# Two merged transformer layers on one core: index-head weights inside a projection panel, paired index scores, a first panel in pieces, and an output made token by token

## The chip, the cores and the metric

One core of a Trainium2 chip runs the whole kernel, in one launch. The metric is the device time in microseconds; smaller is better. A run's time lies some 2 us above the span that its trace shows from the first to the last instruction.

## The reference, cut to what matters

Input x has 512 tokens of width 1024, all in fp32. A first layer (sliding-window and differential attention, then a feed-forward part with a short convolution) is followed by a second one:

```python
xn = rms_norm(x, norm_gain)
z = xn @ w_in
q, c_kv, q_idx, k_idx, w_idx, g_attn, x_rnn, g_rnn, merge = split_cols(z)   # 1024,128,512,64,8,1024,1024,1024,2048
c_kv = rms_norm(c_kv, kv_norm_gain)
k_idx = layer_norm(k_idx, idx_ln_gain, idx_ln_bias)
s_idx = relu(einsum('btjd,bsd->btjs', q_idx, k_idx))          # 8 index heads of width 64
s_idx = einsum('btjs,btj->bts', s_idx, w_idx)                 # causal, then the 128 best keys of each token
o = attention over the chosen keys, 16 heads
mixed = sigmoid(merge_a) * ((o * silu(g_attn)) @ w_attn_proj) + sigmoid(merge_r) * (rg_lru(...) @ w_rnn_proj)
x = x + mixed @ w_out
return rms_norm(x, final_norm_gain)
```

The norm at the end is over the width of each token. The matrix products run in a split form: each operand is a rounded fp32 high part and a low part, and a product is three matmuls, high x high, high x low, low x high.

## The kernel before

**Panels.** All weights come as 100 panels of 128 x 2048 fp32 (1 MB), in the order of `STAGES`: in1 (3), fill1, out1, the feed-forward stages up0 to dn3, then in2a (7), xr, rg, wr, ga, mga, ap, out2 (4). SyncE loads panel p into `RAW[p % 2]`, one transfer each, once the low half of panel p - 2 is done. ScalarE rounds it to the high half `WH` (`hi`, L889; for panel p + 2 when TensorE has finished panel p: `hi_ahead`). VectorE (L1341) or, for stages not in `LO_STAGES`, GpSimd (L334, four pieces) makes the low half `WL`. TensorE's `one_panel` (L341) does 48 matmuls of 128x512 per panel: two output tiles m, eight chunks c of the contraction, three passes (L354 to L356). Its outputs are two of the four banks of `PG`, alternating with the panel, and a panel begins when its low half is there and the panel two before it is evacuated by VectorE. Where `ready` is given the order is chunk by chunk, so that each chunk of the activations (high `XH` by ScalarE, low `XL` by VectorE) can arrive while the panel runs.

**The start.** SyncE issues the columns `COL` (200 KB of vectors), panel 0, two slices of x, panel 1; ScalarE issues the other two slices of x. TensorE waits for panel 0 to land, runs 14 warm-up matmuls (`keep_warm`, L406), then panel 0. ScalarE squares x (L951), VectorE adds the four pairs (`add_pairs`, L1318) and TensorE sums over the partitions with two fp32 matmuls against a constant (`mean_square`, L400), after panel 0. `factor` turns the sum into R, by which every evacuation is multiplied. The norms n3 and n5 do the same a quarter of the way into the second panel that follows.

**in2a.** Panel 0 of in2a holds the latent and, twice, the index key (64 columns and their copy); panels 1 and 2 the index queries, 3 to 6 the queries. After panel 1 TensorE does `kv_sums` (mean of the key, mean square of the latent), `w_idx` (the eight index weights of all tokens, 24 matmuls with 8 output columns, L708 to L710) and `ln_sums`. `idx_scores(u)` (L743 to L745) is one index head of one block of 128 query tokens: three matmuls on 64 rows against 256, 384 or 512 keys. The 24 units stand one by one after the chunks of panels 3 and 4 that `IDX_PLACES` names; ScalarE takes the relu from four `PX` banks (L1165) and VectorE adds it, weighted, to the mask `MD` (L1745).

**The attention scores** (`mla_scores`, L822) of a head pair are two fp32 matmuls, one on rows 0 to 63 and one on rows 64 to 127, into different banks. An fp32 matmul leaves two records.

**The end.** ap (L354 with `RH`, `OLO`) gives the attention's part; VectorE gates it (L1990), adds the recurrence's part (L1993) and makes the low part (L1328). out2 has features on the partitions: VectorE adds x, reloaded into `XT` (L2001), ScalarE squares; after the last panel come four mean-square matmuls with warm-up ones between them, the logarithm and exponential of `factor`, and eight scalings `SQ2` (L2005) with a store for every two.

**The form of dn3.** The last feed-forward stage puts tokens on the partitions (`down_panel`): each of two column halves is two panels, each with half the contraction, and the token tiles end one after the other in the second. VectorE adds a tile (L1716), ScalarE squares it with a running sum (L930) and takes the root (L945), and VectorE's `token_factor` makes the tile's factor (L1568 to L1574).

## Time and profile before

| | |
|---|---|
| three runs | 1342.82, 1342.91, 1340.68 us, median 1342.82 |
| the profiled execution | 1342.5 us, span 1340.4 us |
| TensorE busy | 1312.2 us (98%), granted clock 0.996 of full |
| VectorE, ScalarE, GpSimd busy | 838.2, 576.4, 217.1 us |
| high half of a panel, ScalarE | 1.91 us |
| low half of a panel | 2.29 us on VectorE, 5.0 to 6.8 us on GpSimd |
| a slice of x, 128x512 | 0.71 us high (ScalarE), 0.75 us low (VectorE) |
| last low parts before out2 (L1328) | 1282.41 to 1289.29 |

Each time in the trace counts from the first instruction. One engine that is busy nearly all of the span sets the end; the others matter where TensorE waits for them. Matmuls are pipelined: the distance of their starts is their cost, and the duration of one (0.39 us for 128x512) is longer than that.

### The profile page before, as it was taken

How to read it: one execution, taken by the hardware profiler on the slowest of the kernel's cores; microseconds unless marked ns; L12 is line 12 of the kernel's file. 1: busy time of each engine (PE TensorE's matmuls, PEld its weight loads, DVE VectorE, ACT ScalarE, POOL GpSimd, SP SyncE). 2: the span in 40 equal slices, each digit the busy share in tenths (PEclk: the TensorE clock that was granted, in tenths of full speed). 3: DMA queues.
4: the chain of work that ended last, by engine and by line, in shares of the span. 5: the costliest groups of instructions: out<-in, count | busy, mean ns of one | idle time of the engine just before them, and what ended most of it. 6: DMA issues, size and time to landing. Idle time of an engine off the chain costs nothing.

```text
span 1340.4 us, 16043 instructions
## 1 busy us (share of the span) xinstructions
PE 1312.2 (98%) x5982; PEld 1023.7 (76%) x5982; DVE 838.2 (63%) x1450; ACT 576.4 (43%) x871; POOL 217.1 (16%) x173
## 2 busy tenths in 40 slices
PE   7999998999999999999999999999999999999996
PEld 6777677888888888888888876687778866668885
DVE  6455765898887388648853554688886356642333
ACT  5344766544443244224422463224573256654221
POOL 1333320000000000000000032340005411123550
PEclk9999999999999999999999999999999999999998
DMA  5211111232222222222222140322122210002411
GB/s 199 95 63 64 34 61 63 73 116 94 94 94 94 94 94 98 103 107 99 96 95 94 63 158 32 126 94 95 63 98 90 95 64 32 32 33 95 157 64 63
DMA packets 17787, 116.51 MB, mean 87 GB/s; under 512 B 1984, under 2 KB 2240, under 8 KB 4544
## 3 DMA queue, kind: packets, MB, share of 16 engines
q1 hardware_dynamic: 16320, 108.35, 22.8%
q10 hardware_dynamic: 1408, 7.37, 1.5%
q8 instruction: 38, 0.62, 0.2%
q14 instruction: 21, 0.17, 0.0%
HBM read 111.52 MB, written 4.19 MB: 86 GB/s over the span
## 4 chain that ended last, share of the span: by engine, by line
PE 97%; ACT 1%; DVE 1%; DMA 0%; issue 0%; DVEq 0%; ACTq 0%; SPq 0%
PE PG L354 19%; PE PG L356 19%; PE PG L355 19%; PE PX L506 5%; PE PX L793 4%; PE PG L441 2%; PE PX L441 2%; PE PX L440 2%; PE PG L442 2%; PE PG L440 2%; PE PX L442 2%; PE PG L822 2%; PE PX L832 1%; PE PX L689 1%; PE PG L574 1%; PE PX L520 1%
## 5 line engine op out<-in xcount | busy, mean ns | idle before, releaser
L354 PE MATMUL PG<-XH,WH 128*128 128x512 f32 x992 | 393.1, 396 | 2.7 <-DVE XL L1606 2.7
L334 POOL TENSOR_TENSOR WL<-RAW,WH 128x512 fp32r<-128x512 f32 x160 | 213.8, 1369 | 1090.7 <-ACT WH L889 1090.7
L355 PE MATMUL PG<-XL,WH 128*128 128x512 f32 x992 | 386.2, 389 | 0.0
L356 PE MATMUL PG<-XH,WL 128*128 128x512 f32 x992 | 386.2, 389 | 0.0
L889 ACT ACTIVATE WH<-RAW 128x2048 fp32r<-128x2048 f32 x100 | 191.4, 1914 | 346.1 <-PE PG L356 234.4
L354 PEld LDWEIGHTS PG<-XH,WH 128*128 128x128 f32 x992 | 186.2, 188 | 48.6 <-issue 10.0
L355 PEld LDWEIGHTS PG<-XL,WH 128*128 128x128 f32 x992 | 186.3, 188 | 39.2 <-issue 1.9
L356 PEld LDWEIGHTS PG<-XH,WL 128*128 128x128 f32 x992 | 186.2, 188 | 38.9
L1341 DVE TENSOR_TENSOR WL<-RAW,WH 128x2048 fp32r<-128x2048 f32 x60 | 137.2, 2287 | 61.0 <-ACT WH L889 60.9
L1094 ACT ACTIVATE Z<-Z 128x512 f32<-128x512 f32 x32 | 20.3, 633 | 164.8 <-DVE Z L1657 164.8
L1641 DVE TENSOR_TENSOR U<-PG,R 128x1024 f32<-128x1024 f32 x32 | 39.2, 1224 | 51.5 <-PE PG L356 46.0
L440 PE MATMUL PX<-WH,AH 128*128 128x512 f32 x128 | 49.8, 389 | 0.0
L441 PE MATMUL PX<-WH,AL 128*128 128x512 f32 x128 | 49.8, 389 | 0.0
L442 PE MATMUL PX<-WL,AH 128*128 128x512 f32 x128 | 49.8, 389 | 0.0
L440 PE MATMUL PG<-WH,AH 128*128 128x512 f32 x128 | 49.8, 389 | 0.0
L441 PE MATMUL PG<-WH,AL 128*128 128x512 f32 x128 | 49.8, 389 | 0.0
L442 PE MATMUL PG<-WL,AH 128*128 128x512 f32 x128 | 49.8, 389 | 0.0
L354 PE MATMUL PG<-RH,WH 128*128 128x512 f32 x128 | 49.8, 389 | 0.0
L356 PE MATMUL PG<-RH,WL 128*128 128x512 f32 x128 | 49.8, 389 | 0.0
L1082 ACT ACTIVATE C<-U,COL 128x512 f32<-128x512 f32 x64 | 48.2, 800 | 0.1
L1652 DVE SCALAR_TENSOR_TENSOR C<-U,COL,C 128x510 f32<-128x510 f32 x64 | 45.1, 747 | 3.8
L1648 DVE SCALAR_TENSOR_TENSOR C<-U,COL,C 128x511 f32<-128x511 f32 x64 | 45.0, 744 | 0.0
(311 smaller groups left out, 2015.9 us busy)
## 6 DMA issues: line engine op xcount, KB each, us to landing
RAW<-panels SPq DMA_DIRECT2D x100, 1024.0 KB, 4.8
x_spill<-XT ACTq DMA_DIRECT2D x1, 2048.0 KB, 7.0
XT<-x_spill ACTq DMA_DIRECT2D x1, 2048.0 KB, 7.9
outT<-SQ SPq DMA_DIRECT2D x4, 512.0 KB, 3.0
XT<-xT ACTq DMA_DIRECT2D x2, 512.0 KB, 6.3
XT<-xT SPq DMA_DIRECT2D x2, 512.0 KB, 8.8
RGW<-rgw ACTq DMA_DIRECT2D x1, 1024.0 KB, 4.8
UK<-uk ACTq DMA_DIRECT2D x1, 512.0 KB, 5.7
```

Source lines behind the costliest of these rows:

```text
L334: ins = pool.tensor_tensor(WL[:, s].rearrange("p a b -> p (a b)")[:, piece], RAW[:, s, piece], WH[:, s].rearrange("p a b -> p (a b)")[:, p ...
L354: pe.matmul(o, WH[:, s, c, ms], xh[:, c, :], start=(c == 0), stop=False)
L355: pe.matmul(o, WH[:, s, c, ms], xl[:, c, :], start=False, stop=False)
L356: mm = pe.matmul(o, WL[:, s, c, ms], xh[:, c, :], start=False, stop=(c == DC - 1))
L440: pe.matmul(o, ah, wh, start=(half == 0 and c == 0), stop=False)
L441: pe.matmul(o, al, wh, start=False, stop=False)
L442: mm = pe.matmul(o, ah, wl, start=False, stop=(half == 1 and c == 3))
L506: mm = pe.matmul(PX[:, 2, :], w[:, s, c, m * P:(m + 1) * P], x[:, c, :], start=(c == 0 and w is WH and x is XH), stop=(c == DC - 1 and w i ...
L793: mm = pe.matmul(PX[:, 2, :], w[:, s, c, m * P:(m + 1) * P], x[:, c, :], start=(c == 0 and w is WH and x is XH), stop=(c == DC - 1 and w i ...
L889: act.activation(WH[:, s].rearrange("p a b -> p (a b)"), RAW[:, s, :], ACT.Copy).then_inc(w_hi, 1)
L1082: ins = act.activation(C[:, b, m, :], U[:, b, m, :], ACT.Identity, bias=col("cb", k + 32 * m), scale=col("cw2", k + 32 * m))
L1341: dve.tensor_tensor(WL[:, s].rearrange("p a b -> p (a b)"), RAW[:, s, :], WH[:, s].rearrange("p a b -> p (a b)").bitcast(F32), ALU.subtrac ...
```

## The change

- **in2a.** The first panel's columns are the latent, the index key once, the eight index weights and 56 zeros. `w_idx` and its loads and splits go. VectorE evacuates the latent, copies the key to both row halves and scales the weights out of the panel. `kv_sums` moves inside panel 1, behind 39 of its 48 matmuls, `ln_sums` behind 12 matmuls of panel 2. ScalarE's squares stand ahead of the high half of panel 3.
- **Index scores.** A visit does two heads, on the two row halves, with the three passes interleaved; 12 visits.
- **The mean squares.** VectorE adds the last two tiles too, and one matmul sums them. For n1 it moves from behind panel 0 to behind 12 matmuls of panel 1.
- **The start.** Panel 0 comes in three pieces (512, 512 and 1024 columns), with high and low halves per piece; the columns and three slices of x are issued by ScalarE. Sixteen warm-up matmuls wait for the constants alone. The high half of panel 2 stands ahead of the first norm's factor on ScalarE. The recurrence's scales (`lru_scales`, some 20 small operations on VectorE) move behind the first evacuation.
- **The end.** out2 has the form of dn3. Reloaded x is transposed by TensorE during panels 2 and 3 of ap (16 transposes each), ScalarE copies it to `X3T`, and the gain comes as a 128 x 1024 tile. Each token tile is scaled by its own factor and stored in two halves of 256 KB. The output leaves as 512 x 1024, without the host's transposition.

```diff
-        IDX_PLACES = {3: {4 + n: n for n in range(12)}, 4: {2 + n: 12 + n for n in range(12)}}
+        IDX_PLACES = {3: {4 + 2 * n: n for n in range(6)}, 4: {2 + 2 * n: 6 + n for n in range(6)}}
...
-            sp.dma_start(COL[:], cols_in).then_inc(loaded_c, 16)
-            sp.dma_start(RAW[:, 0, :], panels[0]).then_inc(raw_in[0], 16)
-            for k in range(0, 4, 2):
-                sp.dma_start(XT[:, 2 * k:2 * k + 2, :], xT_chunks(k)).then_inc(loaded_x[k], 16)
+            for q in range(3):
+                piece = slice(512 * q, 512 * q + 512 if q < 2 else 2048)
+                sp.dma_start(RAW[:, 0, piece], panels[0][:, piece]).then_inc(raw_in[0] if q == 2 else first_in[q], 16)
+            sp.dma_start(XT[:, 4:6, :], xT_chunks(2)).then_inc(loaded_x[2], 16)
...
+                        if first and c == 2:
+                            pe.wait_ge(once("first_lo"), 2)
+                        if first and c == 4:
+                            pe.wait_ge(w_lo, 1)
...
-                sums = {0: lambda: mean_square(norm, [(acc, 1, src[:, 0, :]), (acc, 1, src[:, 1, :])])}
+                sums = {0: lambda: mean_square(norm, [(acc, 1, src[:, 0, :])])}
...
-            keep_warm(14)
-            gemm_norm("in1", "n1", SQ1, "x1_split")
+            keep_warm(16)
+            acc1 = once("n1_acc")
+            pe.wait_ge(once("first_lo"), 1)
+            one_panel(0, 0, ready=(once("x1_split"), 0), first=True)
+            one_panel(1, 1, quarter_done=lambda: mean_square("n1", [(acc1, 1, SQ1[:, 0, :])]))
...
 
-            def w_idx():
-
-                pe.wait_ge(once("wi_split"), 1)
-                for c in range(DC):
-                    o = PX[0:8, 0, :]
-                    pe.matmul(o, WIH[:, c, :], XH[:, c, :], start=(c == 0), stop=False)
-                    pe.matmul(o, WIL[:, c, :], XH[:, c, :], start=False, stop=False)
-                    mm = pe.matmul(o, WIH[:, c, :], XL[:, c, :], start=False, stop=(c == DC - 1))
-                mm.then_inc(once("wx_ready"), 1)
...
+
+                qb, pair = v // 4 + 1, v % 4
                 n = (qb + 1) * P
-                rows = slice((j % 2) * HD, (j % 2) * HD + HD)
-                if u == 0:
+                if v == 0:
                     pe.wait_ge(once("idx_split"), 2)
-                if u == 3:
+                if v == 1:
                     pe.wait_ge(once("idx_split"), 3)
...
-                    pe.wait_ge(once("idx_relu"), u - 3)
-                qh, ql = (q[rows, j // 2, qb * P:(qb + 1) * P] for q in (QIH, QIL))
-                pe.matmul(PX[:, u % 4, 0:n], qh, KIH[rows, 0:n], start=True, stop=False)
-                pe.matmul(PX[:, u % 4, 0:n], qh, KIL[rows, 0:n], start=False, stop=False)
-                pe.matmul(PX[:, u % 4, 0:n], ql, KIH[rows, 0:n], start=False, stop=True).then_inc(once("idx_s"), 1)
+                if v >= 2:
+                    pe.wait_ge(once("idx_relu"), 2 * v - 2)
+                for k, (q, key) in enumerate(((QIH, KIH), (QIH, KIL), (QIL, KIH))):
+                    for m in range(2):
+                        rows = slice(m * HD, (m + 1) * HD)
+                        mm = pe.matmul(PX[:, (2 * v + m) % 4, 0:n], q[rows, pair, qb * P:(qb + 1) * P], key[rows, 0:n],
+                                       start=(k == 0), stop=(k == 2))
+                        if k == 2:
+                            mm.then_inc(once("idx_s"), 1)
 
             p0 = FIRST["in2a"][0]
             acc = once("n5_acc")
             one_panel(p0, p0 % 2, ready=(once("x3_split"), 0), chunk_done=turn_rest("n4", F4, "x3_new"))
             one_panel(p0 + 1, (p0 + 1) % 2,
-                      quarter_done=lambda: mean_square("n5", [(acc, 1, SQF[:, 0, :]), (acc, 1, SQF[:, 1, :])]))
-            kv_sums()
-            w_idx()
-            ln_sums()
-            one_panel(p0 + 2, p0 % 2)
+                      quarter_done=lambda: mean_square("n5", [(acc, 1, SQF[:, 0, :])]), inner=(1, 4, kv_sums))
+            one_panel(p0 + 2, p0 % 2, quarter_done=ln_sums)
...
-            gemm_sums("out2", "n6", GA, ready=(once("m_split"), 0))
+
...
+
+
+                def turn():
+                    if f == 0:
+                        pe.wait_ge(reloaded, 16)
+                    else:
+                        pe.wait_ge(once("x3_copied"), NB)
+                    for t in range(NB):
+                        for c in range(4):
+                            mm = pe.transpose(PX[:, t, c * P:(c + 1) * P], XT[:, 4 * f + c, t * P:(t + 1) * P], IDN[:])
+                        mm.then_inc(once("x3_turned"), 1)
+
+                return turn
+
+            def last_panel(k):
+
+                p = FIRST["out2"][0] + k
+                f, half = divmod(k, 2)
+                pe.wait_ge(w_lo, p + 1)
+                if k < 2:
+                    pe.wait_ge(once("m_split"), 4 * k + 4)
+                if half == 0:
+                    if f == 0:
+                        pe.wait_ge(once("x3_copied"), 2 * NB)
...
+
+            p0 = FIRST["ap"][0]
+            for k in range(4):
+                one_panel(p0 + k, (p0 + k) % 2, RH, OLO, ready=(once("o_split"), 0) if k == 0 else None,
+                          quarter_done=turn_x3(k - 2) if k >= 2 else None)
+            for k in range(4):
...
+            act.dma_start(COL[:], cols_in).then_inc(loaded_c, 16)
+            for k in (0, 1, 3):
                 act.dma_start(XT[:, 2 * k:2 * k + 2, :], xT_chunks(k)).then_inc(loaded_x[k], 16)
...
+                if k < 2:
+                    act.wait_ge(first_in[k], 16)
+                    act.activation(WH[:, 0, 2 * k:2 * k + 2, :].rearrange("p a b -> p (a b)"),
+                                   RAW[:, 0, 512 * k:512 * k + 512], ACT.Copy).then_inc(once("first_hi"), 1)
+                if k == 2:
+                    act.wait_ge(raw_in[0], 16)
+                    act.activation(WH[:, 0, 4:8, :].rearrange("p a b -> p (a b)"), RAW[:, 0, 1024:2048], ACT.Copy).then_inc(w_hi, 1)
...
             hi(1, 1, 0)
-            squares("n1", SQ1, XT)
+            squares("n1", SQ1, XT, (1, 2, 3))
+            hi_ahead(0)
 
             act.wait_ge(once("lam_dot"), 2)
...
             act.wait_ge(once("ln_x"), 1)
             act.activation(CSQ[:, 1, :], KC[:], ACT.Square).then_inc(once("ln_sq"), 1)
+            hi_ahead(p0 + 1)
...
+                if t in (1, 2):
+                    f = t - 1
+                    if t == 1:
+                        act.dma_start(FG[:], fin_in).then_inc(loaded_f, 16)
+                    for b in range(NB):
+                        act.wait_ge(once("x3_turned"), 4 * f + b + 1)
...
+                    link(dve.tensor_tensor(sq[:, 0:2, :], sq[:, 0:2, :], sq[:, 2 * k:2 * k + 2, :], ALU.add))
+                dve.tensor_tensor(sq[:, 0, :], sq[:, 0, :], sq[:, 1, :], ALU.add).then_inc(once(name + "_acc"), 1)
...
+            for k in range(2):
+                dve.wait_ge(once("first_hi"), k + 1)
+                dve.tensor_tensor(WL[:, 0, 2 * k:2 * k + 2, :].rearrange("p a b -> p (a b)"), RAW[:, 0, 512 * k:512 * k + 512],
+                                  WH[:, 0, 2 * k:2 * k + 2, :].rearrange("p a b -> p (a b)").bitcast(F32), ALU.subtract)\
...
 
-            in2a_out(0, CKV[:])
-            dve.wait_ge(once("wi_hi"), 1)
-            dve.tensor_tensor(WIL[:], WIR[:], WIH[:].bitcast(F32), ALU.subtract).then_inc(once("wi_split"), 1)
-            in2a_out(1, two(QI, 0))
+            dve.wait_ge(panel_done, p0 + 1)
+            dve.tensor_tensor(CKV[:, 0, :], PG[:, 2 * (p0 % 2), :], R[:], ALU.mult).then_inc(once("kv_raw"), 1)
+            for half in (0, HD):
+                ins = dve.tensor_tensor(CKV[half:half + HD, 1, :], PG[0:HD, 2 * (p0 % 2) + 1, :], R[0:HD, :], ALU.mult)
+            ins.then_inc(once("ki_raw"), 1)
+            dve.scalar_tensor_tensor(out=WXT[HD:HD + 8, :], in0=PG[HD:HD + 8, 2 * (p0 % 2) + 1, :],
+                                     scalar=IDX_HEADS ** -0.5 * HD ** -0.5, in1=R[HD:HD + 8, :],
+                                     op0=ALU.mult, op1=ALU.mult).then_inc(evac, 1)
             dve.wait_ge(once("ln_mean"), 1)
-            dve.wait_ge(evac, p0 + 1)
+            dve.wait_ge(once("ki_raw"), 1)
             dve.scalar_tensor_tensor(out=KC[:], in0=PX[:, 3, :], scalar=-1.0, in1=CKV[:, 1, :],
                                      op0=ALU.mult, op1=ALU.add).then_inc(once("ln_x"), 1)
+            in2a_out(1, two(QI, 0))
             dve.wait_ge(once("qi_hi"), 1)
             dve.wait_ge(evac, p0 + 2)
...
-                dve.scalar_tensor_tensor(out=SQ2[:, c, :], in0=M2[:, c, :], scalar=col("final", c), in1=R[:],
-                                         op0=ALU.mult, op1=ALU.mult).then_inc(once("out_ready"), 1)
+            dve.wait_ge(once("x3_copied"), 2 * NB)
+            for m in range(2):
+                if m == 0:
+                    dve.wait_ge(once("dn_tile"), 26)
+                else:
...
+            def store(t, f):
+                fs = slice(f * S, (f + 1) * S)
+                dve.scalar_tensor_tensor(out=OT[:, t, fs], in0=X3T[:, t, fs], scalar=RTK[:, 3 * t + 2:3 * t + 3],
+                                         in1=FG[:, fs], op0=ALU.mult, op1=ALU.mult).then_inc(once("out_ready"), 1)
+
+            for t in range(NB):
+                if t < 3:
+                    dve.wait_ge(once("dn_tile"), 28 + t)
+                else:
+                    dve.wait_ge(panel_done, p0 + 4)
+                dst = X3T[:, t, S:]
+                dve.scalar_tensor_tensor(out=dst, in0=PG[:, t, :], scalar=0.5, in1=dst, op0=ALU.mult, op1=ALU.add)\
+                    .then_inc(once("tok_y") if t < 3 else evac, 1 + t // 3)
+                if t == 1:
+                    first_half("n6")
+                    dve.wait_ge(loaded_f, 16)
+                if t in (1, 2):
+                    token_factor("n6", t - 1)
+                    store(t - 1, 0)
+                    store(t - 1, 1)
+            token_factor("n6", 2)
+            store(2, 0)
+            token_factor("n6", 3)
+            store(3, 0)
+            store(3, 1)
+            store(2, 1)
 
...
+        panel(np.concatenate([ckv, ki, wi, np.zeros((1024, 56), np.float32)], 1)), panel(qi), panel(q2), panel(xr), inter(gr, mg[:, 1024:]), panel(a["w_rnn_proj_2"]),
+        panel(ga), panel(mg[:, :1024]), panel(a["w_attn_proj_2"]), halves(a["w_out_2"]),
```

## Rows read from the trace of the kernel before

**Rows 1.** The page, part 4: the chain that ended last, by engine.
```profile
PE 97%; ACT 1%; DVE 1%; DMA 0%; issue 0%; DVEq 0%; ACTq 0%; SPq 0%
```

**Rows 2.** Timeline of VectorE in ap: start us, us, instruction, xcount, idle before.
```profile
1269.07 1.22 DVE L1990 SCALAR_TENSOR_TENSOR SG<-MGA,PG 128x1024 f32<-128x1024 f32 x1 [4.93 <-PE PG L356]
...
1279.94 1.22 DVE L1990 SCALAR_TENSOR_TENSOR SG<-MGA,PG 128x1024 f32<-128x1024 f32 x1 [4.92 <-PE PG L356]
```

**Rows 3.** Timeline of the start.
```profile
1.33 0.29 POOL L307 TENSOR_SCALAR_AFFINE_SELECT IDN<-IDN 128x128 f32<-128x128 f32 x1 [0.24 <-POOL IDN L305]
...
8.01 5.31 PE L406 MATMUL PX<-O 128*128 128x128 f32 x28 [8.01 <-DMA RAW<-panels]
...
10.16 5.02 ACT L971 ACTIVATE XH<-XT,COL 128x512 fp32r<-128x512 f32 x8 [0.35 <-DMA XT<-xT]
...
13.08 0.47 PE L354 MATMUL PG<-XH,WH 128*128 128x512 f32 x1
...
19.55 3.74 DVE L1318 TENSOR_TENSOR SQ<-SQ 128x1024 f32<-128x1024 f32 x3
```

**Rows 4.** Busy time per stretch: PE, PEld, DVE, ACT, POOL; clock, DMA share, GB/s.
```profile
8.50:9.00 0.50, 0.50 (x4) 0.50 (x3) 0.00 (x0) 0.50 (x1) 0.00 (x0) 1.00 1.06 401
...
4.00:5.00 1.00, 0.00 (x0) 0.00 (x0) 0.00 (x0) 0.00 (x0) 0.41 (x3) 1.00 1.08 426
```

**Rows 5.** DMA issues of 0 to 40 us: count, size, median us to landing.
```profile
COL<-cols SPq DMA_DIRECT2D x1, 200.0 KB, 3.0
```

**Rows 6.** Timeline around the mean square of n5.
```profile
776.18 3.74 DVE L1318 TENSOR_TENSOR SQF<-SQF 128x1024 f32<-128x1024 f32 x3
...
780.91 1.88 PE L400 MATMUL PX<-SQF,O 128*128 128x512 f32 x4
...
782.86 0.40 PE L355 MATMUL PG<-XL,WH 128*128 128x512 f32 x1
```

**Rows 7.** Timeline of TensorE between panels 1 and 2 of in2a.
```profile
790.84 1.02 PE L715 MATMUL PX<-CKV,O 128*128 128x512 f32 x2
...
799.20 0.40 PE L355 MATMUL PG<-XL,WH 128*128 128x512 f32 x1
```

**Rows 8.** Timeline of ScalarE: the second step of the factor R for n5.
```profile
784.83 0.63 ACT L926 ACTIVATE R<-R 128x512 f32<-128x512 f32 x1
```

**Rows 9.** Timeline of TensorE: four visits of the index scores.
```profile
815.35 0.38 PE L743 MATMUL PX<-KIH,QIH 64*128 64x256 f32 x1
...
816.80 0.39 PE L743 MATMUL PX<-KIH,QIH 64*128 64x256 f32 x1
...
841.47 0.49 PE L743 MATMUL PX<-KIH,QIH 64*128 64x512 f32 x1
...
843.25 0.50 PE L743 MATMUL PX<-KIH,QIH 64*128 64x512 f32 x1
```

**Rows 10.** Timeline of TensorE in the attention: score pairs and transposes.
```profile
1092.00 0.70 PE L822 MATMUL PG<-KT,QT 64*128 64x256 f32 x4
1092.63 0.50 PE L793 MATMUL PX<-XH,WH 128*128 128x512 f32 x1
...
1094.12 1.03 PE L689 MATMUL PX<-IDN,PM 128*128 128x128 f32 x8
1095.08 0.92 PE L822 MATMUL PG<-KT,QT 64*128 64x384 f32 x4
```

**Rows 11.** Timeline of VectorE: weighted additions while GpSimd works.
```profile
836.27 3.94 DVE L1745 SCALAR_TENSOR_TENSOR MD<-RLU,SM,MD 128x384 f32<-128x384 f32 x3 [1.05 <-ACT RLU L1165]
```

**Rows 12.** Timeline of the end.
```profile
1323.25 0.39 PE L356 MATMUL PG<-XH,WL 128*128 128x512 f32 x1
...
1331.56 5.39 DVE L2005 SCALAR_TENSOR_TENSOR SQ<-M,COL,R 128x512 f32<-128x512 f32 x8 [6.66 <-ACT R L926]
```

**Rows 13.** Timeline of VectorE at the end of dn3: last tile.
```profile
758.50 0.69 DVE L1716 TENSOR_TENSOR F<-PG,F 128x512 f32<-128x512 f32 x1 [1.13 <-PE PG L442]
...
760.30 0.16 DVE L1571 RECIPROCAL SM<-SM 128x1 f32<-128x1 f32 x1
```

More of the change, by code:

```diff
@@ L340, in _, with one_panel @@
         def _(pe):
-            def one_panel(p, s, xh=XH, xl=XL, ready=None, chunk_done=None, quarter_done=None, between={}, inner=None):
-                pe.wait_ge(w_lo, p + 1)
+            def one_panel(p, s, xh=XH, xl=XL, ready=None, chunk_done=None, quarter_done=None, between={}, inner=None,
+                          first=False):
+                if not first:
+                    pe.wait_ge(w_lo, p + 1)
                 if not (isinstance(p, int) and p < 2):
@@ L877, in _, with turn_x3 @@
                 one_panel(FIRST["mga"][0] + k, (FIRST["mga"][0] + k) % 2, quarter_done=last_values if k == 1 else None)
-            gemm("ap", RH, OLO, ready=(once("o_split"), 0))
-            gemm_sums("out2", "n6", GA, ready=(once("m_split"), 0))
+            def turn_x3(f):
+                def turn():
[11 more added lines that the diff above has]
+                f, half = divmod(k, 2)
+                pe.wait_ge(w_lo, p + 1)
+                if k < 2:
[4 more added lines that the diff above has]
+                    else:
+                        pe.wait_ge(evac, p - 2)
+                for t in range(NB):
+                    o = PG[:, t, :] if f else PX[:, t, :]
+                    ts = slice(t * P, (t + 1) * P)
+                    for c in range(4):
+                        wh, wl = (w[:, p % 2].rearrange("p a b -> p (a b)")[:, c * S:(c + 1) * S] for w in (WH, WL))
+                        xh, xl = (x[:, 4 * half + c, ts] for x in (XH, XL))
+                        pe.matmul(o, xh, wh, start=(half == 0 and c == 0), stop=False)
+                        pe.matmul(o, xl, wh, start=False, stop=False)
+                        mm = pe.matmul(o, xh, wl, start=False, stop=(half == 1 and c == 3))
+                    if half == 1 and t < NB - 1:
+                        mm.then_inc(once("dn_tile"), 1)
+                mm.then_inc(panel_done, 1)
+            p0 = FIRST["ap"][0]
[3 more added lines that the diff above has]
+            for k in range(4):
+                last_panel(k)
         @block.scalar
@@ L947, in token_factors, with squares @@
                 hi_ahead(ahead)
-            def squares(name, dst, src):
-                for k in range(4):
+            def squares(name, dst, src, parts=range(4)):
+                for k in parts:
                     act.activation(dst[:, 2 * k:2 * k + 2, :], src[:, 2 * k:2 * k + 2, :], ACT.Square)\
@@ L981, in _ @@
             factor("n1", R[:])
-            for p in range(3):
+            for p in range(1, 3):
                 hi_ahead(p)
@@ L1159, in _ @@
             for k in range(3, 7):
-                for u in IDX_PLACES.get(k, {}).values():
+                for u in [2 * v + m for v in IDX_PLACES.get(k, {}).values() for m in range(2)]:
                     n = (u // 8 + 2) * P
@@ L1815, in _ @@
             for t in range(3, 7):
-                for u in IDX_PLACES.get(t, {}).values():
+                for u in [2 * v + m for v in IDX_PLACES.get(t, {}).values() for m in range(2)]:
                     idx_add(u)
```

176 lines of the change are left out of this document (77 added, 99 removed).

## The prediction

> **What bounds the kernel now.** Read first the chain that ended last: it lies on TensorE for 97% of the span [rows 1], so a matmul taken away is time taken away, wherever the others keep up. Then the timeline around the places that the change touches. A panel (48 matmuls) takes 10.87 us, from one evacuation to the next, 0.227 us a matmul [rows 2]. Three places count: the start, what TensorE does besides the panels, and the tail. I sum against the profiled execution, 1342.5 us with a span of 1340.4; the median of the runs is 0.3 above it.
>
> **1. The start.** Before, TensorE waits 8.0 us for panel 0's weights, one transfer of 1 MB, then warms up with 28 records in 5.31 us; the slices of x are split from 10.16 on, and the first real matmul starts at 13.08 [rows 3]. The warm-up is slow at first, 4 records in half a microsecond [rows 4]; at the quick pitch (0.11 each) 28 would take 3 us, so some 4.3 us pass before it is reached. The granted clock reads 1.00 all along; the pitch is the better witness. After, it has 32 records and waits for nothing but the constants, which GpSimd finishes at 1.62 [rows 3]: it runs to 1.7 + 5.31 + 4 x 0.11 = 7.5. The data: the queues move 0.4 MB/us at their best [rows 4]. The 200 KB of columns landed 3.0 us after their issue [rows 5]; the first piece of 256 KB is now issued first and should land near 3.7; x's first slices stand second on ScalarE's queue, behind 0.2 MB, and land near 6.1 if both queues share the rate. Then a high and a low slice, 0.7 each: the first matmul could start at 7.6, the warm-up just over. I take 7.7, a gain of 5.4. Bounds: 7.5 (the warm-up) and 11.6 (x as late as the 10.16 of before).
>
> The first panel then runs by chunks of 1.36 us. ScalarE has in order piece 0, XH 0 and 1, piece 1 (0.6), XH 2 and 3 (that x lands near 9), the last half (1.1), XH 4 to 7: XH 2 near 9.8, XH 7 near 14. VectorE follows with 0.66 a slice; chunk 2 is late by 0.2. ScalarE squares two slices before panel 1's high half, which ends near 16.9, its low half (2.29) near 19.2, while TensorE ends panel 0 at 18.8: 0.4 late. The sum of squares moves behind 12 matmuls of panel 1, to 22.0. The three additions take 3.74 [rows 3] after 19.2, the new fourth, of half the width, about 0.65: 23.6. **A new stall of 1.6 us**; behind it in TensorE's queue stands the rest of panel 1. It then needs one matmul in place of two (part 2: 0.86 less). Start: 5.4 + 0.86 - 0.2 - 0.4 - 1.6 = **4.1 us**. The recurrence's scales (5 us of small VectorE operations) move behind the first evacuation, and delay only the second one, which nobody awaits before panel 2 is done: free.
>
> **2. One matmul less in each mean square.** From 780.91 to the second panel matmul at 782.86 are 1.95 us, 1.72 more than the pitch, for two fp32 matmuls [rows 6]: 0.86 each. In the two later norms (n3, n5) one goes: **1.7 us**. Its cover: VectorE's additions began at 776.18 and lasted 3.74 [rows 6]; with the fourth they end near 780.6, and TensorE comes at 780.91. The margin is 0.3; without it the gain shrinks by the lateness, 0.7 at most for the pair.
>
> **3. The index weights inside in2a's first panel.** From the key's mean at 790.84 to the second matmul of the next panel at 799.20 [rows 7] are 8.36, less the pitch 8.1. Three fp32 matmuls in it stay (2.6); the 24 with eight output columns go, and the panel that now carries them keeps its 48 matmuls. **5.5 us.** The sums move: the key's and the latent's behind 39 matmuls of the second panel, near 787.9 in the old time. R is ready at 785.46 [rows 8] less 0.86; three VectorE operations of 0.7 give the latent and both halves of the key at 786.7. Slack 1.2. The centred key's square is ready near 790.2, its sum is due near 794.4. ScalarE's high half stands behind these, but waits for the end of the second panel anyway. The key's split ends near 801.2; the scores that need it come 3.7 us into a panel that starts near 803.5. Nothing becomes late.
>
> **4. Index scores in pairs.** Before, a head's three matmuls stand between two chunks of a panel. From one visit to the next are 1.45 us at 256 columns and 1.78 at 512 [rows 9]; less the chunk's 0.68 a visit costs 0.76 and 1.10, at 384 columns 0.92 between them. Of that 0.32, 0.48 and 0.64 is matmul time, and 0.44 each time the change between 64-row and 128-row work. After, two heads on different row halves share a visit, and 24 visits become 12. Whether the halves run side by side shows in the attention scores, fp32 pairs on the same two halves: four records take 0.63 until the next line starts [rows 10]. In turn they would need 4 x 0.21 = 0.85; side by side 0.43, and 0.2 for the change. So a pair costs one. I add 0.03 a visit for weight loads: 4 x (0.76 + 0.92 + 1.10) - 0.4 = **10.7 us**. Bounds: in turn, only 12 changes go, 12 x 0.44 = 5.3; above 11.1. The Trainium skill (TensorE: Matmul & The Clock Gate, Measured speedup vs the span model) has a speedup of 3.07 for four row tiles; an estimate with that share, 1.54 for two, would leave 7.5 of the 11.5 us of matmuls instead of 5.8 and make this term 9.0. No row shows such a loss.
> Who must keep up: VectorE adds two tiles a visit. Beside GpSimd three additions took 3.94, 1.3 each [rows 11], against a period of 2.1 to 2.5 for two: late by a few tenths during the 6 us of one low half, and the four banks give a visit of slack. No stall.
>
> **5. The end.** TensorE starts its last panel matmul at 1323.25 and ends it 0.39 later; sums, a table load and the scalings follow, which start at 1331.56 and last 5.39; the span ends at 1340.4 [rows 12]: 16.8 us. After, the last projection is made token by token, and only the last tile's factor is open. The same form stands at the end of the feed-forward part: the last tile's addition at 758.50, the reciprocal of its root at 760.30 [rows 13], the factor 0.65 later, and one new step of 0.2. In that time VectorE also makes tile 2's factor and a store. Its queue: addition 0.7, factor of tile 2 0.9, a scaling 0.66, factor of tile 3 0.95, three scalings 2.0: 5.2 us. Before, 3.4 us passed from the last scaling (1336.95) to the end, with transfers of 512 KB; with 256 KB I take 2.9. Tail 8.1, so 8.7 saved; bounds 7.5 to 9.5. **What it costs:** 32 transposes in TensorE's queue, in two panels of ap. Eight take 0.96 with the change of kind [rows 10], so 16 take 1.95: 3.9 us. Their source, the reloaded x, is asked for 20 us ahead; ScalarE's copies (8 of 0.6) fit, since it is busy 4 of a panel's 10.9 us. The split of the mixed tiles, whole now before the second half panel, ended at 1289.3 against 1279.94 + 10.87 = 1290.8 [rows 2]: margin 1.5. **4.8 us net.**
>
> **Sum.** 4.1 + 1.7 + 5.5 + 10.7 + 4.8 = 26.8; 1342.5 - 26.8 = 1315.7; with 0.3 for the median of before, **1316.0 us**.
>
> **Rivals.**
> *Pairs in turn* (0.12): the pairs in rounded fp32 don't overlap; the term is 5.3 and the time 1316.0 + 5.4 = 1321.4. For it: the trace has overlap only for fp32 pairs, alone in their visit. Against: the same row halves, and banks of their own.
> *The start gives half* (0.12): x lands near 9, or the panel stalls on its chunks, 2 to 3 us: 1318.5. For it: x came last of all before, at 10.16 [rows 3]. The Trainium skill (DMA: Bandwidth & Descriptors, Measured) advises transfers of 1 MiB and more and has 138 GB/s for 64 KB; at that rate 256 KB take 1.9 us by an estimate, inside the 3.0 of the row, so that the pieces cost little.
> *A wait takes the place of the index weights* (0.04): R or the key's halves come after 787.9, or part 2's margin is negative, and TensorE stands 3 us at the sums: 1319.
> *The change does not do what its diff says* in one part, say no shorter tail because the stores queue up (0.01): 1321.
>
> **How the numbers follow.** The forecast has 0.68, with a spread of 3 us either way (start 2, end 1, scores 1). The range reaches up to the pairs in turn and down to the better bounds: 1310.5 to 1322.5. A measurement here tells 0.2%, 2.7 us, from no change; all cases but the clock's lie far below 1340: faster 0.96, same 0.01, slower 0.03.
>
> **What will show it.** First panel matmul at 7.7; a stall of 1 to 2 us at the first mean square; no matmul with 8 output columns, and no wait of TensorE for the key; visits of 0.8, 0.95 and 1.1 us with six matmuls; 1.95 us for 16 transposes; 8.1 from the last matmul to the end. The prediction is wrong if visits take 1.1 to 1.7, if x lands after 8, or if TensorE waits for the key's halves.

## The result, and the profile after

The changed kernel takes **1321.93 us** (median, 1320.51 to 1322.39) beside 1342.76 for the kernel before in the same session; the ratio is 0.9847, 95% interval 0.983 to 0.9864, clear of no change. Its profiled execution has a span of 1319.9 us, 20.5 less than before. Forecast were 26.8 us of gain and a time of 1316.0.

Where the 6 us went is read by one kind of row: the moment at which VectorE begins to evacuate a given panel. Here are four such rows of the kernel before (the third panel of in1, the third of in2a, the fifth of in2a, the first of ap), and then the same four of the kernel after. Columns: start us, duration us, instruction, idle before.

```profile
47.81 1.23 DVE L1445 TENSOR_TENSOR PROJ<-PG,R 128x1024 f32<-128x1024 f32 x1 [9.47 <-PE PG L356]
...
810.06 1.23 DVE L1780 TENSOR_TENSOR QI<-PG,R 128x1024 f32<-128x1024 f32 x1 [5.55 <-PE PG L356]
...
854.79 1.23 DVE L1780 TENSOR_TENSOR QT<-PG,R 128x1024 f32<-128x1024 f32 x1 [0.20 <-PE PG L356]
...
1247.31 1.22 DVE L1990 SCALAR_TENSOR_TENSOR SG<-MGA,PG 128x1024 f32<-128x1024 f32 x1 [9.65 <-PE PG L356]
```

```profile
50.43 1.23 DVE L1487 TENSOR_TENSOR PROJ<-PG,R 128x1024 f32<-128x1024 f32 x1 [6.08 <-PE PG L362]
...
805.52 1.23 DVE L1827 TENSOR_TENSOR QI<-PG,R 128x1024 f32<-128x1024 f32 x1 [1.31 <-PE PG L362]
...
839.39 1.22 DVE L1827 TENSOR_TENSOR QT<-PG,R 128x1024 f32<-128x1024 f32 x1
...
1231.89 1.22 DVE L2039 SCALAR_TENSOR_TENSOR SG<-MGA,PG 128x1024 f32<-128x1024 f32 x1 [9.66 <-PE PG L362]
```

The differences are +2.62, -4.54, -15.40 and -15.42. With the rows that answer to [rows 2], [rows 12] and [rows 13] they split the gain:

```profile
760.24 0.69 DVE L1763 TENSOR_TENSOR F<-PG,F 128x512 f32<-128x512 f32 x1 [1.13 <-PE PG L439]
...
1257.95 1.91 PE L878 MATMUL PX<-IDN,XT 128*128 128x128 f32 x16
...
1268.08 1.22 DVE L2039 SCALAR_TENSOR_TENSOR SG<-MGA,PG 128x1024 f32<-128x1024 f32 x1 [6.70 <-PE PG L362]
...
1311.17 0.39 PE L903 MATMUL PG<-WL,XH 128*128 128x512 f32 x1
...
1312.28 0.68 DVE L2069 SCALAR_TENSOR_TENSOR X3T<-PG,X3T 128x512 f32<-128x512 f32 x1
...
1315.33 2.08 DVE L2060 SCALAR_TENSOR_TENSOR OT<-X3T,SM,FG 128x512 f32<-128x512 f32 x3
```

| part | forecast | from the rows |
|---|---|---|
| start, with n1's mean square | -4.1 | +2.62 |
| n3's mean square (758.50 to 760.24: +1.74) | -0.86 | -0.88 |
| n5's mean square and the index weights | -6.36 | -6.28 |
| index scores | -10.7 | -10.86 |
| 32 transposes (-15.42 to -11.86) | +3.9 | +3.56 |
| tail (last panel matmul to end) and last panels | -8.7 | -8.6 |

All lines but the first hold within 0.4 us. The first is wrong by 6.7 us, more than the whole miss. These rows are of one execution; its +2.62 is not the same in every execution of this start, as unpaired will show. At the start of the changed kernel's timeline (rows of engines that don't matter here are left out):

```profile
8.15 1.33 ACT L1000 ACTIVATE XH<-XT,COL 128x512 fp32r<-128x512 f32 x2 [2.72 <-DMA XT<-xT]
...
9.88 0.47 PE L360 MATMUL PG<-XH,WH 128*128 128x512 f32 x1 [2.53 <-DVE XL L1370]
...
22.04 4.84 DVE L1360 TENSOR_TENSOR SQ<-SQ 128x1024 f32<-128x1024 f32 x3
...
22.18 0.50 PE L360 MATMUL PG<-XH,WH 128*128 128x512 f32 x1 [0.92 <-DVE WL L1381]
...
24.53 6.39 POOL L334 TENSOR_TENSOR WL<-RAW,WH 128x512 fp32r<-128x512 f32 x4 [20.13 <-ACT WH L923]
...
26.92 1.64 DVE L1361 TENSOR_TENSOR SQ<-SQ 128x512 f32<-128x512 f32 x1
...
28.61 1.27 PE L406 MATMUL PX<-SQ,O 128*128 128x512 f32 x2 [3.37 <-DVE SQ L1361]
29.17 1.14 PE L360 MATMUL PG<-XH,WH 128*128 128x512 f32 x1
...
30.10 0.63 PE L361 MATMUL PG<-XL,WH 128*128 128x512 f32 x1
30.53 0.63 PE L362 MATMUL PG<-XH,WL 128*128 128x512 f32 x1
```

Four things are to be seen. x's first slices are split from 8.15 on, so the first matmul stands at 9.88 and not at 7.7. Panel 1 waits 0.92 for its low half. The sum of squares is waited for 3.37 us, not 1.6: three additions take 4.84 us (3.74 in [rows 3]) and the fourth 1.64, both beside GpSimd's low half of panel 2. And behind that stall the matmuls stand 0.43 apart instead of 0.23. The busy times per stretch (columns as in [rows 4]; the third number from the end is the granted clock) show why:

```profile
29.00:30.00 1.00, 1.00 (x3) 0.52 (x2) 1.00 (x3) 0.00 (x0) 1.00 (x2) 0.73 0.00 0
30.00:31.00 1.00, 1.00 (x4) 0.71 (x4) 1.00 (x3) 0.00 (x0) 0.92 (x1) 0.50 0.00 0
```

The granted clock is at its lower level, 1.2 GHz, for some 3.4 us. The working theory from here: the start lost its gain to the late x, to the stall at the sum, and to the clock after it.

### The profile page after: what moved, and what is told of

Same layout as the page of the kernel before. It is cut to its first block and busy times, and to the rows that moved or that the text cites. A ratio compares the mean times of both kernels' runs of the same rounds, so it can differ in the third digit from the quotient of the medians.

```text
span 1319.9 us, 16064 instructions
## 1 busy us (share of the span) xinstructions
PE 1294.5 (98%) x5964; PEld 1018.0 (77%) x5964; DVE 850.3 (64%) x1477; ACT 579.3 (44%) x892; POOL 218.5 (17%) x173
## 5 line engine op out<-in xcount | busy, mean ns | idle before, releaser
L360 PE MATMUL PG<-XH,WH 128*128 128x512 f32 x928 | 368.7, 397 | 6.2 <-DVE XL L1653 2.7
L361 PE MATMUL PG<-XL,WH 128*128 128x512 f32 x928 | 362.3, 390 | 0.0
L362 PE MATMUL PG<-XH,WL 128*128 128x512 f32 x928 | 362.2, 390 | 0.0
L360 PEld LDWEIGHTS PG<-XH,WH 128*128 128x128 f32 x928 | 174.6, 188 | 48.3 <-issue 10.5
L361 PEld LDWEIGHTS PG<-XL,WH 128*128 128x128 f32 x928 | 174.8, 188 | 37.3 <-issue 2.3
L362 PEld LDWEIGHTS PG<-XH,WL 128*128 128x128 f32 x928 | 174.6, 188 | 36.6
```

The costliest lines, as they stand in the source:

```text
L360: pe.matmul(o, WH[:, s, c, ms], xh[:, c, :], start=(c == 0), stop=False)
L361: pe.matmul(o, WH[:, s, c, ms], xl[:, c, :], start=False, stop=False)
L362: mm = pe.matmul(o, WL[:, s, c, ms], xh[:, c, :], start=False, stop=(c == DC - 1))
```

## Experiments on the start

**old_start**: the changed kernel with the start of the kernel before, whole (the changed lines of the first stage, undone in the diff shown ahead, but the fourth addition stays).

> The changed kernel with the whole start of the kernel before: panel 0 as one transfer, the old order of transfers and of ScalarE's and VectorE's work, the first norm's sum behind panel 0, the recurrence's scales ahead of the first evacuation. The one matmul less in the mean square stays. Theory (the new start costs time where 4.1 us of gain were forecast): the third panel is evacuated at 47.81 - 0.86 = 46.95 in place of 50.43, so 3.5 us less: 1318.4 us. Rival (the later milestone of the new start is made up for further on, in what it has already done by then): 1321.9 or more.

Measured: 1318.84 us (ratio to before 0.9826, 0.9811 to 0.9841); third panel at 47.06. At the third panel the theory holds to 0.1 us (46.95 was expected), in the time to 0.4: as written, the new start costs 3.1 us, where the forecast had it gain.

**sum_late**: only the place of n1's sum in panel 1.

```
-one_panel(1, 1, quarter_done=lambda: mean_square("n1", ...))
+one_panel(1, 1, inner=(1, 1, lambda: mean_square("n1", ...)))
```

> The changed kernel with one edit: the first norm's sum of squares stands behind 30 matmuls of panel 1, not behind 12. Theory (the start was lost to the stall at that sum, and to the lower clock after it): the additions end at 28.6 as before, TensorE reaches the sum at about 29.2, so the stall of 3.4 us goes and the granted clock stays at 1.00, where it was 0.50 between 30 and 32 us: 3.4 and 1.9 us, so about 1316.6 us, and the third panel is evacuated near 45.1 in place of 50.43. Rival (the stall only hides another wait: the third panel's low half or the reciprocal root come no earlier): panel 2 waits for them at 34 and the gain is under 2 us, 1320 or more.

Measured: 1318.64 us (0.9838, 0.9822 to 0.9853), so 3.3 less in the medians; the third panel comes at 48.43. That median flatters: three executions take 1318.4 to 1318.6 and two 1321.86 and 1322.92, as much as the changed kernel, and the ratio hardly moved. In the profiled execution, one of the three (1318.41), the clock doesn't fall at all before the tail. Both are half right. TensorE no longer waits for the sum, and here the clock stays up. But a wait that had been hidden now shows, for the first evacuation, which needs the root R (ScalarE ends it at 35.6):

```profile
28.66 1.23 DVE L1438 CUSTOM_DVE_ANT_0 R<-LV 128x64 f32<-128x64 f32 x1
29.18 1.02 PE L406 MATMUL PX<-SQ,O 128*128 128x512 f32 x2
...
34.99 0.63 ACT L947 ACTIVATE R<-R 128x512 f32<-128x512 f32 x1
...
37.26 0.47 PE L360 MATMUL PG<-XH,WH 128*128 128x512 f32 x1 [2.94 <-DVE PROJ L1483]
```

**warm_fill**: the stall stays, only the idleness goes.

```
-quarter_done=lambda: mean_square("n1", ...)
+quarter_done=lambda: (keep_warm(14), mean_square("n1", ...))
```

> The changed kernel with 28 more warm-up records (128 columns each, into a bank that nobody reads) ahead of the first norm's sum, where TensorE stands for 3.4 us: 28 x 0.11 is 3.1 us. The stall stays, only its idleness goes. Theory (the slow matmuls after the stall are the granted clock, which falls because TensorE idled): the clock reads 1.00 from 29 to 33 us, the matmuls there take 0.227 each and the time falls by 1.9 us, to about 1320.0. Rival (the slow matmuls come from VectorE's and GpSimd's work beside them, or the clock falls at this place whatever TensorE does): no change, 1321.9.

Measured: 1320.46 us (0.9833, 0.9819 to 0.9846), 1.5 less where 1.9 were expected; the third panel comes at 48.91, also 1.5 earlier. In its busy times the same microsecond reads 1.00, with six matmuls and not four, while VectorE and GpSimd are as busy as before, so the slow matmuls are not their doing:

```profile
30.00:31.00 1.00, 1.00 (x6) 0.80 (x5) 1.00 (x1) 0.00 (x0) 0.99 (x1) 1.00 0.00 0
```

One profile alone would not show that the idleness calls the fall. That all executions lie about 1.5 us lower (1319.01 to 1320.63 for 1320.51 to 1322.39) speaks for it, and so does bridge below.

**late_hi**: `hi_ahead(0)` back behind n1's factor, so that GpSimd starts later.

> The changed kernel with ScalarE's high half of panel 2 back behind the first norm's factor. GpSimd then makes no low half beside VectorE's additions. Theory (the two engines slow each other): the three additions take 3.74 and not 4.84, the fourth 0.69 and not 1.64, the sum comes 2.0 us earlier, the stall is 1.3 us and the clock stays up. But the high half then ends near 31 and the low half near 37.6, while panel 1 ends near 34.5: TensorE waits about 3 us there, so the time stays near 1321 (1319 to 1324). Rival (the additions are slow for a reason of their own): they stay at 4.84 and 1.64, the stall at 3.4, and the later low half comes on top: 1324 or more.

Measured: 1321.08 us (0.9839, 0.9824 to 0.9854). VectorE's and TensorE's rows; GpSimd isn't at work until 33.4:

```profile
22.20 3.74 DVE L1359 TENSOR_TENSOR SQ<-SQ 128x1024 f32<-128x1024 f32 x3
...
25.97 0.69 DVE L1360 TENSOR_TENSOR SQ<-SQ 128x512 f32<-128x512 f32 x1
...
26.71 0.70 PE L406 MATMUL PX<-SQ,O 128*128 128x512 f32 x1 [1.37 <-DVE SQ L1360]
...
38.41 0.80 PE L360 MATMUL PG<-XH,WH 128*128 128x512 f32 x1 [2.37 <-POOL WL L334]
```

3.74, 0.69 and a stall of 1.37 as expected: GpSimd's low half was 2.0 us of the 3.37. The price also came as expected, as TensorE waits 2.37 for the low half of panel 2; behind this wait the granted clock falls (0.50 in 39 to 41 us), which the expectation had left out. Moving that high half ahead was no mistake; the change had put work beside it that suffers. The Trainium skill (GPSIMD Engine Reference, Specifications) says that GpSimd shares its SBUF interfaces with VectorE and contends with instructions that have two SBUF inputs; these rows agree, with 1.64 for 0.69.

**early_dots**: sum_late, and the chain to R shortened.

```
-lo(1, 2); add_pairs("n1", SQ1, 3); <lambda products, small operations>
+<lambda products, small operations>; lo(1, 2); add_pairs("n1", SQ1, 3)
-squares("n1", SQ1, XT, (0,)); hi(1, 1, 0); squares("n1", SQ1, XT, (1, 2, 3))
+hi(1, 1, 0); squares("n1", SQ1, XT)
```

> The kernel sum_late with VectorE's lambda products and the small operations behind them ahead of the low half of panel 1, where VectorE idled 1.95 us, and all four squares behind ScalarE's high half of panel 1. In sum_late TensorE ends panel 1 at 34.3 and waits 2.94 us for the first evacuation, which waits for the reciprocal root R at 35.7: between the sum at 30.2 and R lie the two products on VectorE (1.23 and 1.32 us beside GpSimd), their exponentials and two table loads. Theory (R is late by that chain): R comes 2.7 us after the sum, near 31.6, the wait of 2.94 goes, panel 1 starts 0.9 earlier, the third panel is evacuated near 44.6 in place of 48.43, and the time is near 1315.0 us. Rival (R is set by the sum and the tables alone, or GpSimd's low half of panel 2 ends later than the root): at most 1 us is gained, 1317.6 or more.

Measured: 1316.61 us (0.9807, 0.9791 to 0.9823); third panel at 44.84, near the 44.6 of the theory. TensorE's wait is 0.19, the products take 0.22 each where they had taken 1.23 and 1.32. The time missed by 1.6 us, and that has a place of its own: the clock falls at 207 to 211 us, where sum_late's profile has no fall. The fastest of its four executions took 1314.99, the 1315.0 that was expected.

**x_order**: sum_late, and the first transfers in another order (k: pieces of panel 0; a, b: x's first two slices).

```
-SP: k0, k1, k2, x[2], panel 1     ScalarE: COL, x[0], x[1], x[3]
+SP: k0, a, x[1], x[2], panel 1    ScalarE: COL, b, k1, k2, x[3]
```

> The kernel sum_late with another order of the first transfers: x's first two slices one on each queue, behind 256 and 200 KB, then x's second pair, and the later pieces of panel 0 on the other queue; panel 1 behind all of x. Until x's first pair has landed 1.0 MB is asked for ahead of or beside it, and not 1.4. Theory (x came late because other transfers shared its time): x's first pair lands near 7.0 and not 8.2, the first panel matmul starts near 8.9 and not 9.9, x's last pair near 13.5 and not 15.8; as panel 1 and the root R hang on VectorE's chain behind x's last slices, that chain comes 1 to 2 us earlier: 1316.6 to 1317.6 us. Rival (transfers of 256 KB with rows of 2 KB are slow in themselves, whatever their order): x's first pair lands at 8 or later, and the time stays at 1318.6.

Measured: 1319.63 us (0.983, 0.9814 to 0.9847). ScalarE's and TensorE's first rows, then a stretch of the busy times of the changed kernel and the same of x_order:

```profile
6.36 1.34 ACT L1002 ACTIVATE XH<-XT,COL 128x512 fp32r<-128x512 f32 x2 [1.03 <-DMA XT<-xT]
...
8.10 0.47 PE L360 MATMUL PG<-XH,WH 128*128 128x512 f32 x1 [0.35 <-DVE XL L1372]
```

```profile
4.00:5.00 1.00, 1.00 (x6) 1.00 (x6) 0.00 (x0) 0.41 (x2) 0.40 (x3) 1.00 0.77 161
```

```profile
4.00:5.00 1.00, 1.00 (x6) 1.00 (x6) 0.00 (x0) 0.96 (x2) 0.40 (x3) 1.00 0.99 366
...
36.00:37.00 1.00, 1.00 (x6) 0.82 (x5) 0.96 (x2) 0.00 (x0) 1.00 (x1) 1.00 0.00 0
37.00:38.00 1.00, 1.00 (x5) 0.77 (x4) 0.97 (x2) 0.00 (x0) 1.00 (x2) 0.56 0.00 0
```

On the transfers the theory holds and more: x is there at 6.4, the first matmul comes 1.9 us earlier than in sum_late, and the queues move 366 and not 161 GB/s (the last number of a row) with pieces of the same 256 KB. So pieces of this size are not slow in themselves. The edit also sends x's first pair as two pieces over both queues, and the runs don't separate that from the order; why the rate dips in the old order stays open. On the time it failed: panel 2 starts 1.6 us earlier (35.66), after the same stall of 2.94 us, and this time the clock falls behind it and takes 1.65 back; the third panel comes at 48.48 (sum_late: 48.43). The rest of the difference lies near 211 us, where this profile has a fall and sum_late's has none. So the comparison with sum_late's median is one of clock falls more than of transfers.

**bridge**: the changed kernel and `keep_warm(9)` ahead of `high_chunk(7, ...)`, near 210 us.

> The changed kernel with 18 warm-up records (9 fp32 matmuls of 128 columns into a bank that nobody reads) ahead of the last but one chunk of the attention's output projection, where TensorE stands 2.3 us for a low slice of the mixed heads, near 210 us. In four of the six profiles read so far the granted clock falls to 0.50 for some 3 us after that stall, with the change and without, and in two it does not. Theory (the idleness calls the fall, and each fall costs 1.6 us): no fall near 212 us in the profile, and in no run of it; the median falls by 1.0 to 1.6 us, to 1320.3 to 1320.9 us. Rival (the fall comes from what the other engines do there): it is still seen, 1321.9 us.

Measured: 1320.63 us (0.983, 0.9816 to 0.9843). TensorE, then the clock at 214 us, after and in bridge:

```profile
210.27 2.17 PE L412 MATMUL PX<-O 128*128 128x128 f32 x18
...
212.72 0.50 PE L520 MATMUL PG<-WH,XH 128*128 128x512 f32 x1 [0.28 <-DVE XL L1563]
```

```profile
214.00:215.00 1.00, 1.00 (x4) 0.72 (x4) 0.00 (x0) 0.00 (x0) 0.00 (x0) 0.50 0.00 0
```

```profile
214.00:215.00 1.00, 1.00 (x6) 0.83 (x5) 0.00 (x0) 0.00 (x0) 0.00 (x0) 1.00 0.00 0
```

The fall is gone with the idleness, and the time by 1.3 us. Its executions still lie in two groups, 1318.6 to 1319.0 and 1320.6 to 1320.8. The stall at the sum is still in this kernel, and its profile, of the slower group, has the fall at 29 to 32 us; that the faster ones lack it is not shown.

**best**: sum_late, early_dots, x_order and bridge together.

> The changed kernel with all that helped or should: the first norm's sum behind 30 matmuls of panel 1, the lambda products and VectorE's small operations ahead of panel 1's low half, ScalarE's squares behind panel 1's high half, x_order's order of transfers, and the warm-up records of the kernel bridge. Theory (x_order's first matmul 1.9 us and panel 1 1.6 us earlier were given back by a clock fall after a stall of 2.94 us, and early_dots has taken that stall away): panel 1 starts near 19.7 us, the third panel is evacuated near 43.3 and not 44.84, no clock fall before the last ten microseconds: 1313.3 us. Rival (panel 1's weights land too late in that order, or the root R waits for something else): the third panel is evacuated at 44.8 or later, 1315 or more.

Measured: **1313.37 us**, 0.9783 of the kernel before (0.9769 to 0.9796) and 8.6 us under the changed one. All five executions lie between 1313.28 and 1313.61.

```profile
8.01 0.47 PE L360 MATMUL PG<-XH,WH 128*128 128x512 f32 x1 [0.63 <-DVE XL L1372]
...
19.91 0.50 PE L360 MATMUL PG<-XH,WH 128*128 128x512 f32 x1 [0.41 <-DVE WL L1383]
...
32.22 0.47 PE L360 MATMUL PG<-XH,WH 128*128 128x512 f32 x1 [0.19 <-DVE PROJ L1485]
...
43.40 1.23 DVE L1489 TENSOR_TENSOR PROJ<-PG,R 128x1024 f32<-128x1024 f32 x1 [0.95 <-PE PG L362]
```

The third panel comes at 43.40, 4.4 us ahead of the 47.81 of the kernel before: the 4.1 us that were forecast for the start can be had, but with further edits.

## Experiments on the other parts

**unpaired**: the changed kernel with one head a visit.

```
-IDX_PLACES = {3: {4 + 2 * n: n for n in range(6)}, 4: {2 + 2 * n: 6 + n for n in range(6)}}
+IDX_PLACES = {3: {4 + n: n for n in range(12)}, 4: {2 + n: 12 + n for n in range(12)}}
```

> The changed kernel with the index scores one head a visit, 24 visits, as in the kernel before. Theory (pairs run side by side on the two row halves and cost one head's visit): the five or six panels with the scores take 10.9 us more, 1332.8 us. Rival (pairs in turn, only the changes of kind were saved, and the rest of the gain at that place came from elsewhere): 5.3 us more, 1327.2.

Measured: 1332.69 us (0.9929, 0.9912 to 0.9946), 10.8 more; between the third and the fifth panel of in2a (803.58 and 848.34) its profile takes 44.76 us for the 33.87 of the changed kernel, 10.9 more. Pairs run side by side. The share of 1.54 that the prediction worked out from the Trainium skill (TensorE: Matmul & The Clock Gate, Measured speedup vs the span model) would have made the term 9.0; these runs don't agree with it.

The start of this kernel is that of the changed kernel, instruction for instruction, and yet its profile has the third panel at 48.45 and not at 50.43. Two stretches of its busy times:

```profile
10.00:12.00 2.00, 2.00 (x5) 1.58 (x6) 1.11 (x2) 0.76 (x3) 0.00 (x0) 0.55 1.10 415
...
28.00:30.00 2.00, 2.00 (x9) 1.36 (x8) 2.00 (x5) 0.00 (x0) 2.00 (x3) 1.00 0.00 0
```

Here the clock fell at 10 us, behind the wait of 2.05 us for x, and not behind the stall at the sum. The time that it cost went largely into waits that are missing in turn: panel 1 has its low half in time, and the stall at the sum is 2.16 and not 3.37, also because the three additions took 3.74 (the last section says why). So the same code lost 0.64 us at its start in this execution and 2.6 to 2.8 in the profiles of after, bridge, head_by_head and old_end.

**head_by_head**: two heads a visit, the first head's three matmuls ahead of the second's.

```
-for k, (q, key) in enumerate(...):
-    for m in range(2):
+for m in range(2):
+    for k, (q, key) in enumerate(...):
```

> The changed kernel with 12 visits of two heads, but the first head's three matmuls ahead of the second head's three, where the changed kernel takes them in turn, one of each. Theory (two matmuls overlap only when neighbours in TensorE's queue lie on different row halves): just one place in each visit has such neighbours, so the visits take nearly the time of six matmuls in a row: 12 visits at 2 of 3 matmul times lost, 4 x (0.21 + 0.32 + 0.43) = 3.9 us more, 1325.8 us. Rival (the hardware overlaps them in either order): 1321.9.

Measured: 1322.04 us (0.9846, 0.9829 to 0.9862): no loss, and the theory falls. TensorE's rows show both heads' first matmuls starting together although three are issued before the second head's, and from one visit to the next are 2.15 us in both kernels (809.70 to 811.85 here, 809.40 to 811.55 in the changed one):

```profile
809.70 0.39 PE L734 MATMUL PX<-KIH,QIH 64*128 64x256 f32 x2
809.92 0.29 PE L734 MATMUL PX<-KIL,QIH 64*128 64x256 f32 x2
810.04 0.28 PE L734 MATMUL PX<-KIH,QIL 64*128 64x256 f32 x2
```

**index_only**: the kernel before with the index part alone (w_idx and its weights gone, the columns in in2a's first panel, the sums moved).

> The kernel before with one part of the change alone: the index heads' weights as columns of the first panel of the second layer's input projection in place of the key's copy, the 24 matmuls with eight output columns gone, the key's and the latent's sums inside the next two panels. Theory (24 small matmuls and the waits around them): 5.5 us less, 1337.3 us. Rival (the sums, moved inward, make TensorE wait for R or the key's halves, since here the mean square still takes two matmuls and R comes 0.86 us later): 3 us of it are lost, 1340 us.

Measured: 1337.58 us (0.9959, 0.9943 to 0.9974), 5.1 less in the medians. In its profile the third panel of in2a comes at 805.08 for 810.06, and the last tile of dn3 in front of it at 759.00 for 758.50: 5.5 us, as forecast. TensorE doesn't wait at the sums.

**old_end**: the changed kernel with the end of the kernel before.

> The changed kernel with the end of the kernel before: the last projection in four feature panels, its norm summed at the end, no transposes of x and no token factors; the norm's sum takes three matmuls, not four. Theory (tail 9.1 shorter, two groups of transposes 3.56 and the last panels 0.46 longer): 5.1 us more less the 0.6 for the matmul that is saved here too, 1326.4 us. Rival (the token form gains only what its transposes cost): 1322 us.

Measured: 1326.06 us (0.9874, 0.9858 to 0.9889), 4.1 more against 4.5 expected. The expectation counts the tail of the changed kernel from VectorE's last tile; counted from the last panel matmul, the tail is 8.4 shorter and the last panels 0.2, with the same sum of 8.6.

## Why the prediction was right and wrong

**Right, and for its reasons:** the index weights (5.5 for 5.5, index_only), the pairs (10.8 to 10.9 for 10.7, unpaired), the one matmul less (0.88 for 0.86), the transposes (3.56 for 3.9). All were counts of instructions times durations of [rows 6 to 10], on an engine that never waits there.

**Right, but partly by luck: the tail**, 8.3 us (the last panel matmul ends at 1311.56, the span at 1319.9) for 8.1. Two errors cancel. VectorE takes up the last tile only at 1312.28, 0.7 after that matmul, because it is still busy with the scalings of tile 1; the forecast had it free. And from the last scaling's end at 1317.41 to the end of the span are 2.5, not 2.9. The 5.1 between them were forecast as 5.2. So the tail gave 8.4 of the 8.7, and the last four panels, which the forecast left as they were, gave the 0.2 that is left.

**Wrong: the start**, 4.1 of gain for 2.6 of loss in the profiled execution, so that the time missed by 5.9 us and stayed inside the range only by the width that the pairs gave it. Four steps of the sum failed:

- "x's first slices should land near 6.1": ScalarE gets them at 8.15, past the 8 that the forecast itself named as a sign of being wrong. The queues' rate was taken at its best, 0.4 MB/us. In the order of the change it dips to 161 GB/s; x_order shows 366 with the same bytes. Price 2.2 us (9.88 for 7.7).
- Late chunks in panel 0 and the wait of panel 1 were 0.6 in the sum. From 9.88 to 22.18 are 12.3 us, 1.4 more than a panel's 10.87; price 0.8 us.
- "The three additions take 3.74, the new fourth about 0.65": they take 4.84 and 1.64. Both durations came from rows where GpSimd is still, while the step moved in the same change (ScalarE's high half of panel 2 ahead of the factor) puts GpSimd's low half beside them. [Rows 11] had the contention in view, and it was used for the scores only. Price 1.8 us, the stall 3.37 for 1.6 (2.0 us by late_hi).
- The clock was a rival for the scores alone. It fell at the start, behind a stall that the sum itself forecast: 1.5 us by warm_fill. Whether and where it falls differs from execution to execution (unpaired).

These give 2.2 + 0.8 + 1.8 + 1.5 = 6.3 of the 6.7; the rest is not settled. The rival that the start gives half named the right place and the first two of these steps, but priced them at 2.5 us.

## What to carry to other kernels

When a change moves a step of one engine, ask which engine that releases, and take the durations of all that then lies beside it from rows with that neighbour at work. Where a sum forecasts a new stall of TensorE, add a possible clock fall behind it, and either move the waited work or fill the stall with matmuls that nobody reads. And remove waits in the order of the chain: sum_late and x_order each gave back part of their gain to the next wait or its clock, and only together with early_dots did all of it arrive.

## What the runs showed of the hardware

- **The same stall may or may not cost the clock.** The stall of 2.3 us near 210 us, the same in every kernel but bridge and best, is followed by a stretch at 0.50 in ten of twelve profiles (before and after among them), and by none in sum_late and late_hi; a fall costs 1.6 us (the distance between after and sum_late grows from 1.99 us, 212.47 and 210.48, to 3.61, 228.02 and 224.41, across it). 2.94 us of stall kept the clock in sum_late and lost it in x_order; 2.05 us, the wait for x, lost it in unpaired, and 2.98 at the same place kept it in bridge. The Trainium skill (TensorE: Matmul & The Clock Gate, Part 1: The HAM clock gate) says that the activity monitor runs free of the program, so that one kernel meets it at different phases; the rows agree. It would also explain why executions of one kernel lie up to 4.5 us apart, as in sum_late, and those of best, with no stall above 1.4 us between its first panel and its tail, within 0.33; as only one execution of each kernel was profiled, this is not shown.
- **Which of VectorE and GpSimd starts first decides what the neighbour costs.** In after, GpSimd's first piece starts at 24.53 and VectorE's third addition 0.02 us behind it: it takes 2.33 us for the 1.23 of the others. In unpaired the addition starts at 24.66, 0.11 us ahead of the piece, and takes 1.23; the piece takes 2.23 instead of 1.27. In early_dots, too, a piece that starts while an addition runs leaves it alone. This is why three additions take 4.84 us in some profiles and 3.74 in others. The first row below is after's, the second early_dots':

```profile
24.55 2.33 DVE L1360 TENSOR_TENSOR SQ<-SQ 128x1024 f32<-128x1024 f32 x1
...
24.68 1.45 POOL L334 TENSOR_TENSOR WL<-RAW,WH 128x512 fp32r<-128x512 f32 x1 [20.28 <-ACT WH L923]
```

- **Small VectorE operations suffer most beside GpSimd.** In late_hi's and sum_late's timelines operations of 128x8 take 1.15 to 1.22 us where they take 0.17 alone, as if each waited for a piece of GpSimd's work to end (sum_late's rows):

```profile
37.50 5.04 POOL L334 TENSOR_TENSOR WL<-RAW,WH 128x512 fp32r<-128x512 f32 x4 [6.44 <-ACT WH L923]
37.67 1.15 DVE L1461 TENSOR_TENSOR SM<-SM 128x8 f32<-128x8 f32 x1
38.85 1.22 DVE L1462 TENSOR_SCALAR SM<-SM 128x8 f32<-128x8 f32 x1
```

- **Matmuls on the two row halves overlap in either order of issue**, up to three apart (head_by_head: 2.15 us from visit to visit in both orders).
